# Where the gain of an RMSNorm is multiplied in, in a two-layer decoder kernel with routed experts

## What is computed

```
def rms_norm(x, g):
    y = x * rsqrt(mean(x * x, axis=-1) + EPS)
    return y * g

def hierarchical_moe(h, r_grp, r_exp, w_gate, w_up, w_down):
    ...                                  # gates: 2 of 16 experts per token
    a = einsum("td,edf->tef", t, w_gate)
    u = einsum("td,edf->tef", t, w_up)
    hid = silu(a) * u * gates[:, :, None]
    y = einsum("tef,efd->td", hid, w_down)

for l in range(2):
    x = x + mixer_l(rms_norm(x, g_l))
    h = rms_norm(x, ffn_norm[l])
    x = x + hierarchical_moe(h, ...)
return rms_norm(x, final_norm)
```

## Time and profile before

| what | value |
|---|---|
| median of 3 runs | 1708.24 us |
| lowest and highest | 1705.39 and 1712.94 us |
| the profiled execution's own time | 1705.39 us |
| its span, first to last instruction | 1703.2 us |
| PE busy | 1520.8 us (89%) |
| DVE busy | 1069.7 us (63%) |
| ACT busy | 667.9 us (39%) |
| POOL busy | 385.2 us (23%) |
| mean granted TensorE clock | 0.945 of full |

### The profile page before, as it was taken

One profiled execution on the slowest core, in us unless ns is written; L12 is line 12 of the kernel. 1 busy time (PEld: TensorE's weight loads), 2 busy tenths in 40 slices (PEclk: granted clock), 3 DMA queues, 4 the chain that ended last, 5 costly groups with the idle time before them and its releaser, 6 DMA issues. The chain is left out here.

```text
span 1703.2 us, 19568 instructions
## 1 busy us (share of the span) xinstructions
PE 1520.8 (89%) x7176; PEld 1187.9 (70%) x7176; DVE 1069.7 (63%) x1318; ACT 667.9 (39%) x725; POOL 385.2 (23%) x341
## 2 busy tenths in 40 slices
PE   6889595999999984999999999999989499999991
PEld 5779274667676743888888888888877476767660
DVE  6887535755565538766757677585753665665553
ACT  4110622555555535324243232423322355555532
POOL 3100001322222213522405042240500222222220
PEclk9989795999999996999999999999999599999996
DMA  4213523588888826212112121211203768888854
GB/s 177 77 66 127 200 85 133 185 351 341 359 351 369 351 103 251 87 50 83 56 57 86 37 76 60 74 62 49 86 29 132 316 259 359 347 366 345 350 211 172
DMA packets 52337, 309.75 MB, mean 182 GB/s; under 512 B 10320, under 2 KB 16080, under 8 KB 38480
## 3 DMA queue, kind: packets, MB, share of 16 engines
q1 hardware_dynamic: 34592, 286.03, 42.6%
q0 software_dynamic: 9648, 16.80, 2.7%
q10 hardware_dynamic: 8064, 6.50, 1.2%
HBM read 299.32 MB, written 28.31 MB: 192 GB/s over the span
## 5 line engine op out<-in xcount | busy, mean ns | idle before, releaser
L1253 DVE TENSOR_TENSOR wgl<-WR,wgh 128x2048 fp32r<-128x2048 f32 x66 | 148.6, 2290 | 214.4 <-ACT wgh L793 211.5
L636 POOL TENSOR_TENSOR KQ<-rope_ab 64x512 f32<-64x512 f32 x96 | 173.2, 1804 | 384.5 <-DVE rope_ab L1337 380.9
L1573 PE MATMUL PS<-WR,SC 128*128 128x512 f32 x528 | 233.2, 594 | 3.3 <-ACT SC L830 1.3
L862 ACT ACTIVATE wh<-wraw 128x1024 fp32r<-128x1024 f32 x80 | 84.6, 1058 | 270.2 <-PE PS L1638 247.2
L1573 PEld LDWEIGHTS PS<-WR,SC 128*128 128x128 f32 x528 | 98.8, 190 | 117.2 <-issue 115.1
L1253 DVE TENSOR_TENSOR wul<-WR,wuh 128x2048 fp32r<-128x2048 f32 x66 | 148.0, 2284 | 0.2 <-ACT wuh L793 0.2
L793 ACT ACTIVATE wgh<-WR 128x2048 fp32r<-128x2048 f32 x66 | 122.4, 1904 | 61.4 <-DMA WR<-w_gate 61.4
L793 ACT ACTIVATE wuh<-WR 128x2048 fp32r<-128x2048 f32 x66 | 122.7, 1906 | 30.4 <-PE PS L1543 18.4
L1337 DVE TENSOR_TENSOR rope_ab<-PS,rope_sb 32x512 f32<-32x512 f32 x192 | 131.9, 687 | 2.6
L1318 DVE TENSOR_TENSOR wl<-wraw,wh 128x1024 fp32r<-128x1024 f32 x80 | 98.0, 1225 | 50.0 <-ACT wh L862 48.3
L1541 PE MATMUL PS<-wgh,xgh 128*128 128x512 f32 x264 | 109.4, 415 | 0.0
(11 more groups left out here) (261 smaller groups left out, 3253.4 us busy)
## 6 DMA issues: line engine op xcount, KB each, us to landing
WR<-w_gate SPq DMA_DIRECT2D x33, 2048.0 KB, 12.2
WR<-w_up SPq DMA_DIRECT2D x33, 2048.0 KB, 16.9
WR<-w_down SPq DMA_DIRECT2D x33, 2048.0 KB, 13.0
wraw<-w_qkv SPq DMA_DIRECT2D x72, 512.0 KB, 3.3
WR<-w_in SPq DMA_DIRECT2D x8, 1024.0 KB, 5.0
WO<-w_out SPq DMA_DIRECT2D x1, 4096.0 KB, 16.0
xn_dram<-HTQ SPq DMA_DIRECT2D x8, 512.0 KB, 2.7
HT<-y_dram SPq DMA_DIRECT2D x8, 512.0 KB, 6.7
```

The source lines that it names most:

```text
L636: nc.gpsimd.tensor_tensor(to, cos, sin, ALU.add).then_inc(rope_done, 1)
L862: nc.scalar.activation(wh[:, s, :], wraw[:, s, :], ACT.Copy).then_inc(wh_done, 1)
L1253: V.tensor_tensor(lo[:, kts, :], raw[:, kts, :], hi[:, kts, :].bitcast(F32), ALU.subtract).then_inc(done, 1)
L1573: ins = M.matmul(PS[3 + h][:, :], hidT[:, ft, :], wd[b][:, ft, h * 512:(h + 1) * 512], start=ft == 0, stop=ft == FT - 1)
```

## The change

The gain of the norm ahead of the experts is no longer multiplied into `XN`. `norm_dve` uses the same line for f0 and f1 as for the other norms (`X * rstd`), `gain_row` and its two DMAs are gone, and `vn` grows from 24 to 40 columns. The copies to `HT` take the gain as a scalar for each partition. For the expert rows DVE gets a new step, `copy_xgT`: it reads the transposed rows from PSUM, multiplies by the gain and writes them to an SBUF tile `xgT[b]`. `rows_lead` and `rows_trail` read that tile, with one instruction of 1024 elements in place of two of 512. Both slots of a pair now use banks 5 and 6 for their transposed rows, so `transpose_rows` waits until the other slot's rows have been copied out. The order of DVE ahead of the first turn changes, and `up(0)` no longer waits for the rows of slot 1.

```
-        gain_row = cut(SC, 0, D)
+        xgT = [cut(SC, 2 * D + b * D, KT, P) for b in range(2)]
...
-            sp.dma_start(gain_row, a["ffn_norm"][0].to_broadcast([P, D])).then_inc(row_in.sem, 16)
...
-                        nc.scalar.activation(HT[:, kt, :], PS[kt][:, :], ACT.Copy).then_inc(ht_act.sem, 1)
+                        nc.scalar.activation(HT[:, kt, :], PS[kt][:, :], ACT.Copy, scale=vn[:, V_NORM[k] + kt:V_NORM[k] + kt + 1]).then_inc(ht_act.sem, 1)
...
                 def rows_lead(b, n):
-                    act.wait_ge(xgT_mm[l][b], n)
-                    for q in range(2):
-                        nc.scalar.activation(xgh[b][:, 4 * q:4 * q + 4, :], PS[ROW_BANKS[b][q]][:, :].rearrange("p (a b) -> p a b", a=4),
-                                             ACT.Copy).then_inc(xh_done[l], 1)
+                    act.wait_ge(xgT_done[l][b], n)
+                    nc.scalar.activation(xgh[b][:, :, :], xgT[b], ACT.Copy).then_inc(xh_done[l], 1)
...
-                    elif k in ("f0", "f1"):
-                        if n == 0:
-                            dve.wait_ge(row_in.sem, row_in.at(int(k[1]), 16))
-                        V.scalar_tensor_tensor(XN[k][:, n, :], X[:, n, :], rstd[:, one], gain_row, ALU.mult, ALU.mult).then_inc(xn_ready.sem, 1)
...
-                        V.tensor_copy(HT[:, kt, :], PS[kt][:, :]).then_inc(ht_dve.sem, 1)
+                        V.tensor_scalar(HT[:, kt, :], PS[kt][:, :], vn[:, V_NORM[k] + kt:V_NORM[k] + kt + 1], None, ALU.mult).then_inc(ht_dve.sem, 1)
...
+                def copy_xgT(b, n):
+                    dve.wait_ge(xgT_mm[l][b], n)
+                    for q in range(2):
+                        ins = V.tensor_tensor(xgT[b][:, 4 * q:4 * q + 4, :], PS[5 + q][:, :].rearrange("p (a b) -> p a b", a=4),
+                                              gain[:, 4 * q:4 * q + 4].rearrange("p (a o) -> p a o", o=1).to_broadcast([P, 4, P]), ALU.mult)
+                    ins.then_inc(xgT_done[l][b], 1)
...
                 def rows_trail(b, m):
-                    for q in range(2):
-                        dve.wait_ge(xh_done[l], 2 * m + (q + 1))
-                        ins = V.tensor_tensor(xgl[b][:, 4 * q:4 * q + 4, :], PS[ROW_BANKS[b][q]][:, :].rearrange("p (a b) -> p a b", a=4),
-                                              xgh[b][:, 4 * q:4 * q + 4, :].bitcast(F32), ALU.subtract)
-                    ins.then_inc(xl_done[l], 1)
-
-                gate_trail(0, 0, [0])
-                rows_trail(0, 0)
-                gate_trail(0, 0, [1])
-                rows_trail(1, 1)
+                    dve.wait_ge(xh_done[l], m + 1)
+                    V.tensor_tensor(xgl[b][:, :, :], xgT[b], xgh[b][:, :, :].bitcast(F32), ALU.subtract).then_inc(xl_done[l], 1)
+
+                gate_trail(0, 0)
+                for b in range(2):
+                    copy_xgT(b, 1)
+                for b in range(2):
+                    rows_trail(b, b)
                 up_trail(0, 0)
...
                         copy_hidT(0)
+                        copy_xgT(0, i + 2)
                         gate_trail(0, 2 * i + 2)
...
                         up_trail(0, 2 * i + 2)
+                        copy_xgT(1, i + 2)
                         rows_trail(1, 2 * i + 3)
...
                 def transpose_rows(b, n):
                     pe.wait_ge(gathered[l][b], n * 16)
+                    if b == 1 or not isinstance(n, int):
+                        pe.wait_ge(xgT_done[l][1 - b], n - 1 if b == 0 else n)
                     for kt in range(KT):
-                        ins = M.transpose(PS[ROW_BANKS[b][kt // 4]][:, (kt % 4) * P:(kt % 4 + 1) * P], xg[b][:, kt::KT], ident[:, :])
+                        ins = M.transpose(PS[5 + kt // 4][:, (kt % 4) * P:(kt % 4 + 1) * P], xg[b][:, kt::KT], ident[:, :])
                     ins.then_inc(xgT_mm[l][b], 1)
...
                 def project(dst, b, m, hi, lo, ready):
+                    pe.wait_ge(xl_done[l], m + 1)
...
                     def gate(b):
-                        pe.wait_ge(xl_done[l], 2 * i + (b + 1))
...
                     def up(b):
-                        if b == 0:
-                            pe.wait_ge(xl_done[l], 2 * i + 2)
```

More of the change, by code:

```diff
@@ L69 @@
             + [(0, kt) for kt in range(2, KT)])
-V_NORM = {"a": 0, "kv": 8, "q": 16}
-NORM_COLS = 24
-ROW_BANKS = ((5, 6), (7, 1))
+V_NORM = {"a": 0, "f0": 8, "kv": 16, "q": 24, "f1": 32}
+NORM_COLS = 40
 PREV, OWN, PHASE, OWN_T, PREV_T, PHASE_T = range(6)
@@ L382, in build_program @@
         xgT_mm = [[sem(f"xgT_mm{l}{b}") for b in range(2)] for l in L2]
-        row_in = Count(sem("row_in"), L2, [16] * 2)
+        xgT_done = [[sem(f"xgT_done{l}{b}") for b in range(2)] for l in L2]
         wg_in = [[sem(f"wg_in{l}{b}") for b in range(2)] for l in L2]
@@ L514, in _ @@
             sp.wait_ge(oT_done, 2 * NP_HEADS)
-            sp.dma_start(gain_row, a["ffn_norm"][1].to_broadcast([P, D])).then_inc(row_in.sem, 16)
             sp.dma_start(rt.rearrange("p a b -> p (a b)"), a["router"][1]).then_inc(rt_in.sem, 16)
@@ L1246, in moe_dve, with trail @@
                 last = dve.value_load(last_i[0:1, 0:1], min_val=E // 2 - 1, max_val=(E + XB) // 2 - 1)
-                def trail(raw, hi, lo, lead_done, done, m, qs=range(2)):
-                    for q in qs:
+                gain = vn[:, V_NORM[f"f{l}"]:V_NORM[f"f{l}"] + KT]
+                def trail(raw, hi, lo, lead_done, done, m):
+                    for q in range(2):
                         kts = slice(q * KT // 2, (q + 1) * KT // 2)
@@ L1253, in trail, with gate_trail @@
                         V.tensor_tensor(lo[:, kts, :], raw[:, kts, :], hi[:, kts, :].bitcast(F32), ALU.subtract).then_inc(done, 1)
-                def gate_trail(b, m, qs=range(2)):
-                    trail(wg[b], wgh, wgl[b], gh_done[l], gl_done[l], m, qs)
+                def gate_trail(b, m):
+                    trail(wg[b], wgh, wgl[b], gh_done[l], gl_done[l], m)
                 def up_trail(b, m):
                     trail(wu[b], wuh, wul[b], uh_done[l], ul_done[l], m)
-                def rows_trail(b, m):
-                    for q in range(2):
-                        dve.wait_ge(xh_done[l], 2 * m + (q + 1))
-                        ins = V.tensor_tensor(xgl[b][:, 4 * q:4 * q + 4, :], PS[ROW_BANKS[b][q]][:, :].rearrange("p (a b) -> p a b", a=4),
-                                              xgh[b][:, 4 * q:4 * q + 4, :].bitcast(F32), ALU.subtract)
-                    ins.then_inc(xl_done[l], 1)
-                gate_trail(0, 0, [0])
-                rows_trail(0, 0)
-                gate_trail(0, 0, [1])
-                rows_trail(1, 1)
+                def copy_xgT(b, n):
+                    dve.wait_ge(xgT_mm[l][b], n)
+                    for q in range(2):
+                        ins = V.tensor_tensor(xgT[b][:, 4 * q:4 * q + 4, :], PS[5 + q][:, :].rearrange("p (a b) -> p a b", a=4),
+                                              gain[:, 4 * q:4 * q + 4].rearrange("p (a o) -> p a o", o=1).to_broadcast([P, 4, P]), ALU.mult)
+                    ins.then_inc(xgT_done[l][b], 1)
+                def rows_trail(b, m):
+                    dve.wait_ge(xh_done[l], m + 1)
[5 more added lines that the diff above has]
+                    rows_trail(b, b)
                 up_trail(0, 0)
@@ L1821, in lay_out @@
     a = {"x": f["x"]}
-    a["norm_vecs"] = asc(cat([by_row(f["a_norm"][0]), by_row(f["kv_norm"]), by_row(f["b_norm"][0])], 1))
-    a["ffn_norm"] = f["ffn_norm"].reshape(2, 1, D)
+    a["norm_vecs"] = asc(cat([by_row(f["a_norm"][0]), by_row(f["ffn_norm"][0]), by_row(f["kv_norm"]),
+                              by_row(f["b_norm"][0]), by_row(f["ffn_norm"][1])], 1))
     a["conv_vecs"] = asc(cat([by_tile(f["a_b_in"][0]), by_block, by_tile(f["a_ln_g"][0]), by_tile(f["a_ln_b"][0]), same, taps,
```

## The result

| | before | after |
|---|---|---|
| median | 1708.14 us (5 runs) | 1720.32 us (5 runs) |
| lowest and highest | 1705.39, 1712.94 | 1718.72, 1723.05 |
| ratio, with its 95% interval | | 1.0073 [1.006, 1.0085] |
| the profiled execution | 1705.39 (span 1703.2) | 1721.70 (span 1719.6) |

The change costs 12.2 us by these medians, against 11.8 forecast from the median shown before. Counted so, the change costs 13.5 to 14.2 us, near the +13.5 to which the forecast's parts add up. The page of the changed kernel: span, busy time, and the granted clock in 40 slices.

What follows compares the result with a forecast made beforehand. PE bounds the expert loops; outside them a chain of DVE, ACT and PE does. Terms -2.1 + 0.2 + 11.9 + 3.5 = +13.5 gave 1718.9 profiled, 1721.7 as median; it said 1720 us, range 1710 to 1728.

Steps and rivals of the forecast that it cites:

- The norms: In f0 and f1 the multiplication takes 754 ns, not 1285, so PE starts 1.06 us earlier a layer: -2.1 us.
- the copies to `HT`: In the norms, DVE's four copies with a scalar from `vn` cost +0.1 us a layer: +0.2 us.
- The start of the experts: Ahead of each layer's first turn, five serial steps of weights, copies, transposes and trailing rows delay gate(0): +11.9 us together.
- The clock: At each layer's start PE's standing makes gate(0) run at half speed for 2.9 to 4.7 us: net +3.5 us.
- The loops: In the 15 turns DVE's 2.5 us more a turn fits its idle time, so PE loses nothing: 0.
- The clock up through the norm: Rival: PE stays at 2.4 GHz from projection through norm and router, saving 17 us, so 1703; chance 0.06.

Runs made afterwards that it cites:

- experts_only: The changed kernel with the norm's part undone: gain multiplied in the norm again, `copy_xgT` a plain copy; 1720.94 us, ratio 1.0085 to the kernel before.
- norm_only: The kernel before with the norm's part of the change alone, expert rows left without their gain; 1704.32 us against 1706.79, ratio 0.9989.
- half_first: The changed kernel with DVE copying slot 0's rows after half the weights ahead of the first turn, banks still shared; 1712.85 us.
- banks_apart: The changed kernel with the two slots' transposed rows in banks of their own again, DVE's order as changed; 1715.47 us.
- halves: The changed kernel with banks apart, DVE reordered, and slot 0's copy, leading and trailing rows done in halves of 512; 1709.36 us.
- pe_filled: The changed kernel with useless identity transposes in PE's two gaps at each layer's start, no wait removed; 1716.26 us.
- both: The changed kernel with banks apart and DVE's order half the weights, copy, trailing rows, other half, copy; 1712.11 us, ratio 1.0028 to the kernel before.
- second look: The kernel before, unchanged, profiled once more; 1708.06 us.
- halves_filled: The kernel of halves with useless transposes in PE's idle stretches ahead of the norm's transposes, router and gate(0); 1702.67 us, ratio 0.9978 to the kernel before.

## Why the prediction was right

- **The norms (-2.1).** Right: PE's idle time fell by 1.06 us a layer, 4.13 to 3.07. That the whole 1.06 is kept was wrong: 1.1 us came back, in transposes that ran slower (6.11 to 6.55, 5.2 to 5.45) and in the copies to `HT`, where the forecast had +0.2. The forecast put the router at 0, and it cost 0.75. The profiles show the clock at both places, no run parts them. The three unfilled profiles with the old norm (*experts_only* is one) have f1's router at 11.3 to 11.4 us; of the nine with the cheaper norm six have it at 13.6 to 13.8 and three at 11.0 to 11.3. norm_only bounds the sum: -1.9 us, interval -3.4 to -0.3.
- **The start of the experts (+11.9).** Right, link by link; measured 12.5. half_first and banks_apart each undo one cause and give back some 7 and 3 to 5 us. halves undoes both and also splits the first copy; in its profile gate(0) starts 11.1 us earlier than in the changed kernel, so nearly all.
- **The clock (+3.5).** Right in size, 3.8, and pe_filled gives 4 back with the waits left in. The ground given, that the transposes don't count over the gap, is only part of it: norm_only, both and halves lost 0.9 to 2.7 us a layer against the 5.44 of full clock, behind gaps of 2.1 us and less. The two expectations that took the clock to come back with a shorter gap, those of both and halves, missed by 3 us or more.
- **The loops (0).** Right: no new wait, and twice the copies cost 1.3 us by the medians. They gave back 0.8; the waits for `hidden` in layer 0 shrank by 1.0, where at most 0.4 was expected.
- **The clock up through the norm (a rival).** It fell. In f1 PE did start early enough to find the clock at 2.4 GHz, and it was at 0.50 within 1.3 us, by 1322.6. The ground given against it, that an early start does not keep the clock up, held.
- **The number.** That 1720 was met to 0.3 us is in part luck. The parts that it had too low (copies and transposes 0.9, router 0.75, start 0.6, clock 0.3) and the two at which time came back (0.8 each) partly cancel. The forecast's own sum gave 1721.7 for the median, by way of a median of three executions that the later sets put 1.5 to 2.2 us too high, and it gives no reason for saying 1720.
- **The copy as such.** The Trainium skill (VectorE: DVE Perf Modes, section Rules for kernel authors) advises to copy out of PSUM first where many operations follow. With two readers it bought DVE 0.06 us a slot, 1223 ns against 1.28 us, and ACT, whose leading parts of the 34 slots took 35.7 us in place of 36.6, 0.03.

**What stays open.** How long PE had worked when 2.4 GHz came differs at the start of the experts, counted from slot 0's first transpose: 3.8 and 4.9 us in the kernel before, 3.9 and 5.1 in its second look, but 8.3 and 6.3 in norm_only and 8.1 and 8.8 in halves, at nearly the same work. No run here tells why. Nor is it settled why the router in f1 took 13.8 us in one execution after and 11.0 in the other; it began at a clock of 0.50 in the first and at 1.00 in the second.

## What to carry to other kernels

A copy that moves work off a busy buffer was free inside a loop whose bound engine is another, and cost its whole chain ahead of the first turn, where nothing is in flight yet: price the prologue on its own, instruction by instruction. When buffers are shared to save room, look at who frees them first in that prologue: here the order cost some 7 us and the sharing 3 to 5. A stand of PE can cost more than its length, since the work behind it may run at half clock; work that nobody reads, put into such stands, gave 5 us to a kernel already tuned.

## What the runs showed that was not expected

- The clock can fall while PE is busy, 1.1 us after a block's start and behind a stand of only 1.83 us (*both*, 1364.90 to 1366.00).
- At the start of the experts 2.4 GHz came after 3.8 to 8.8 us of nearly the same work, broken by 1.0 us at most.
- The router's 64 small matmuls gained from filling ahead of them: 13.56 to 10.38 us in f0 (12.44 in *halves_filled*).
